# Three FFN norms with the reciprocal root applied where the gate and up products are read, and the opening's squares taken from token rows

## The chip, the core and the metric

One Trainium2 chip, of which the kernel uses one core. The metric is the device time of one execution in microseconds (us); less is better. TensorE (PE) does the matmuls and has a granted clock of either 1.2 or 2.4 GHz (0.50 or 1.00 in the profile). VectorE (DVE), ScalarE (ACT) and GpSimd (POOL) do elementwise work, SyncE (SP) issues DMA. Each engine runs its own queue in order, and engines wait for each other through semaphores.

## What is computed

A two-layer transformer over 512 latent tokens and 256 context tokens, width 1024, all in float32. Each layer is FFN, token mix, FFN, each with an RMS norm and adaLN modulation in front:

```python
def rms_norm(x, w):
    y = x * rsqrt(mean(x * x, axis=-1) + 1e-6) * w
def modulate(h, shift, scale):
    return h * (1.0 + scale) + shift
def swiglu(h, w_in, w_out):
    gate, up = split(h @ w_in, 2)
    return (silu(gate) * up) @ w_out          # inner width 2816
# per layer; mod = silu(c) @ w_ada + b_ada gives nine vectors of width 1024 each for latent and context
h = h + 0.5 * mod[2] * swiglu(modulate(rms_norm(h, w0), mod[0], mod[1]), ...)   # norm 3*layer
h = h +       mod[5] * token_mix(modulate(rms_norm(h, w1), mod[3], mod[4]))     # norm 3*layer + 1
h = h + 0.5 * mod[8] * swiglu(modulate(rms_norm(h, w2), mod[6], mod[7]), ...)   # norm 3*layer + 2
```

Context tokens have their own modulation vectors. The last FFN (norm 5) has latent tokens only. The result is a last RMS norm of the latent tokens.

## The kernel before

**Layout.** The residual h lies transposed in SBUF: 128 partitions, KD = 8 tiles of the width, TOK = 768 tokens (0 to 511 latent, 512 to 767 context). A norm's output is a pair xhi, xlo (float32r, high part and remainder) of the same shape; an activation is ahi, alo, a weight tile raw becomes whi, wlo. Each product is three passes, whi x xhi, whi x xlo, wlo x xhi, each as one matmul of 512 columns and one of 256 (part_ 0 and 1), into the two banks of a PSUM tensor pg[s]. A *unit* is one output tile of 128 columns; units alternate between slots s = 0 and 1, each with its own pg, raw, whi and wlo.

**Phases** (`phases`): for each FFN two halves of (in, out): 11 steps of one gate unit (slot 0) and one up unit (slot 1) with 8 k-steps each (`unit`, L709), then 8 output tiles of 11 k-steps. The mix is "win" (16 units), `mix`, and "wo" (8 units). In front of the matmuls of a unit TensorE waits for the slot's weights (s_w) and for its pg to have been read (s_free).

**A step of an in phase.** ScalarE (L1414) applies Silu to pg[0] into gate and then makes whi for both slots (split_hi, L1155). VectorE multiplies gate by pg[1] (L1901), copies ahi (L1904), subtracts alo (L1906), and makes wlo (split_lo, L1493), one of them ahead of these and one behind.

**AdaLN pieces.** The later modulation vectors are computed beside the FFNs (ADA_STEPS): 61 of the in steps of norms 0, 2 and 3 (and 3 out steps) carry a piece of w_ada. VectorE multiplies and adds its 16 tiles (sum_ada, L1574 and L1577), eight ahead of the first wlo and eight behind it, and TensorE folds the result over the partitions behind the step's second unit (ada_fold, L724), for which it waits until the last sum. SP loads the piece in four parts, each when its buffer has been summed, in one queue with the weight loads.

**Norms.** Squares are made by ScalarE (square, L1164, square_part, L1176), summed by VectorE into rstd (L1504, L1621) and over the partitions by TensorE against ones (square_sums, L770). ScalarE forms the reciprocal root by Ln and Exp (root, L1235 and L1237; a table load L1248 in front). Then for each k: VectorE tnorm = h * acol * rstd (norm_scaled, L1632), ScalarE xhi = tnorm + shift (L1244), VectorE xlo = tnorm + shift - xhi (L1640).

**Around a norm.** The last pair of units of the phase before is made part by part (last_pair): both slots' 512 latent tokens first, so that their squares can be taken during the 256 context tokens of both slots; add_part (L1612) adds them to h. Then first_pair makes the first two units of the new phase as the k arrive: latent tokens of slot 0 and 1, k = 0 to 3 each, then k = 4 to 7 in turns, then the context tokens slot by slot (part_product, L776).

**Opening** (opening_pair, norm 0). x is transposed on TensorE (L740) and copied to h by ScalarE and VectorE in turns; squares and sums of the 8 k follow. The first 16 tiles of w_ada arrive in four large loads (ada_first0 to 3): for each, first_modulation (L751), a copy to part_first (copy_first, L1202 or L1527), first_fold (L758), read_first into mod and acol. TensorE's queue alternates them with the k-steps of the first unit pair.

**257 columns.** The position DFT (L887) streams rows of dft_sb that are 257 columns long and lie one behind the other; the channel DFT (L853) streams 256 columns. Both are plain float32.

## Time and profile before

| | us |
|---|---|
| median of three runs | 2743.12 (2735.91 to 2744.52) |
| the profiled execution | 2739.12 |
| its span (first to last instruction) | 2737.2 |
| TensorE busy | 2664.7, 97% |
| VectorE busy | 1521.2, 56% |
| ScalarE busy | 692.3, 25% |
| mean granted TensorE clock | 0.992 |

The profile is of one execution. Its page gives busy times by engine; the other views used below are windows (busy time of each engine in a stretch, with the granted clock, the DMA engines' busy share and the GB/s moved), timelines (instructions of one engine in order), and groups of instructions by line, with shapes kept apart. "Idle before" in brackets says how long an engine stood still before an instruction and what released it. Matmul starts are measured, their ends are modelled and overlap; distances between starts are what counts.

### The profile page before, as it was taken

The page shows a single profiled execution, that of the slowest core. Times are in us where ns is not written, and L with a number is a line of the kernel's source. Part 1 is how long each engine was busy: PE and PEld are TensorE (multiplying, and loading weights), DVE is VectorE, ACT ScalarE, POOL GpSimd, SP SyncE. Part 2 cuts the span into 40 slices and gives each one's busy share as a digit, 9 for nine tenths or more (in the row PEclk, how much of TensorE's full clock was granted, in tenths as well). Part 3 has the DMA queues.
Part 4 walks back from the last instruction along what each step waited for, and adds up shares of the span by engine and source line. Part 5 has one row for each costly group of instructions (what it writes and reads, how often), then busy time and mean ns, then how long its engine had stood idle before and what let it go on. Part 6 is the DMA issues. An engine that isn't in the chain of part 4 may idle for free.

```text
span 2737.2 us, 42267 instructions
## 1 busy us (share of the span) xinstructions
PE 2664.7 (97%) x15515; PEld 2290.5 (84%) x15515; DVE 1521.2 (56%) x2621; ACT 692.3 (25%) x1075; POOL 93.7 (3%) x211
## 2 busy tenths in 40 slices
PE   7999999999999999999999999999999989999998
PEld 4888888888877888888888888888887877888886
DVE  5776477534376477626763677247536465543333
ACT  4111111122256221111111311111113345422222
POOL 0000000000034000000000000000000022000000
PEclk8999999999999999999999999999999999999999
DMA  7877477412200177536762577257422200233332
GB/s 228 198 184 185 113 184 184 125 50 79 54 17 2 54 165 185 146 86 159 184 161 58 123 184 175 71 140 184 126 70 84 69 26 17 81 96 100 91 110 81
DMA packets 485795, 316.98 MB, mean 116 GB/s; under 512 B 30588, under 2 KB 483664, under 8 KB 485712
## 3 DMA queue, kind: packets, MB, share of 16 engines
q1 hardware_dynamic: 485712, 315.88, 45.2%
q8 instruction: 51, 0.84, 0.1%
q14 instruction: 32, 0.26, 0.0%
HBM read 313.73 MB, written 2.10 MB: 115 GB/s over the span
## 4 chain that ended last, share of the span: by engine, by line
PE 91%; DVE 4%; ACT 2%; issue 1%; POOL 1%; DMA 0%; SPq 0%; DVEq 0%; ACTq 0%; POOLq 0%
PE pg L709 79%; PE pg L776 4%; PE p L1047 1%; PE pn L1030 1%; PE pg L986 1%; PE p L724 1%; DVE xlo L1640 1%; DVE tnorm L1632 1%; PE pg L867 1%; ACT whi L1155 0%; DVE wlo L1493 0%; PE pg L991 0%; DVE probT L1847 0%; DVE mx L1854 0%; ACT xhi L1244 0%
## 5 line engine op out<-in xcount | busy, mean ns | idle before, releaser
L709 PE MATMUL pg<-xhi,whi 128*128 128x512 f32 (+1 forms) x2856 | 794.5, 347 | 4.1 <-DVE wlo L1493 4.0
L709 PE MATMUL pg<-xhi,wlo 128*128 128x512 f32 (+1 forms) x2856 | 788.6, 344 | 0.0
L709 PE MATMUL pg<-xlo,whi 128*128 128x512 f32 (+1 forms) x2856 | 787.1, 344 | 0.0
L1155 ACT CAST whi<-raw 128x1024 fp32r<-128x1024 f32 (+1 forms) x288 | 321.8, 1118 | 1060.2 <-PE pg L709 1045.9
L1493 DVE TENSOR_TENSOR wlo<-raw,whi 128x1024 fp32r<-128x1024 f32 (+1 forms) x288 | 377.6, 1311 | 350.5 <-ACT whi L1155 347.8
L709 PEld LDWEIGHTS pg<-xhi,whi 128*128 128x128 f32 x2856 | 451.3, 188 | 72.6 <-DVE wlo L1493 5.9
L709 PEld LDWEIGHTS pg<-xlo,whi 128*128 128x128 f32 x2856 | 450.4, 188 | 69.3
L709 PEld LDWEIGHTS pg<-xhi,wlo 128*128 128x128 f32 x2856 | 450.4, 188 | 68.9
L1577 DVE SCALAR_TENSOR_TENSOR part<-ada,cond,part 128x256 f32<-128x256 f32 x960 | 465.3, 485 | 32.7
L1703 DVE SCALAR_TENSOR_TENSOR h<-pg,gcol,h 128x512 f32 (+1 forms) x118 | 71.4, 639 | 442.3 <-PE pg L709 437.5
L709 PE MATMUL pg<-ahi,whi 128*128 128x512 f32 x1100 | 306.1, 346 | 0.0
L709 PE MATMUL pg<-ahi,wlo 128*128 128x512 f32 x1100 | 305.4, 346 | 0.0
L709 PE MATMUL pg<-alo,whi 128*128 128x512 f32 x1100 | 304.4, 345 | 0.0
L1414 ACT ACTIVATE gate<-pg 128x768 f32<-128x768 f32 (+1 forms) x88 | 66.8, 759 | 574.4 <-PE pg L709 574.0
L709 PEld LDWEIGHTS pg<-alo,whi 128*128 128x128 f32 x1100 | 174.0, 188 | 27.7
L709 PEld LDWEIGHTS pg<-ahi,whi 128*128 128x128 f32 x1100 | 174.2, 188 | 27.0
L709 PEld LDWEIGHTS pg<-ahi,wlo 128*128 128x128 f32 x1100 | 173.6, 188 | 26.8
L1901 DVE TENSOR_TENSOR gate<-gate,pg 128x768 f32<-128x768 f32 (+1 forms) x88 | 78.1, 888 | 136.8 <-PE pg L709 136.8
L776 PE MATMUL pg<-xhi,whi 128*128 128x256 f32 (+1 forms) x240 | 85.2, 355 | 9.1 <-DVE xlo L1640 5.6
L1906 DVE TENSOR_TENSOR alo<-gate,ahi 128x768 f32 (+3 forms) x88 | 78.5, 892 | 9.7
L776 PE MATMUL pg<-xlo,whi 128*128 128x256 f32 (+1 forms) x240 | 81.0, 338 | 0.0
L776 PE MATMUL pg<-xhi,wlo 128*128 128x256 f32 (+1 forms) x240 | 80.6, 336 | 0.0
(212 smaller groups left out, 1983.4 us busy)
## 6 DMA issues: line engine op xcount, KB each, us to landing
ada<-in_w_ada SPq DMA_DIRECT2D x512, 256.0 KB, 4.2
raw<-in_ffn_w_in SPq DMA_DIRECT2D x176, 512.0 KB, 3.9
raw<-in_ffn_w_out SPq DMA_DIRECT2D x64, 704.0 KB, 4.5
raw<-in_w_in SPq DMA_DIRECT2D x24, 512.0 KB, 3.8
ada_first<-in_w_ada SPq DMA_DIRECT2D x8, 1024.0 KB, 11.9
raw<-in_w_in SPq DMA_DIRECT2D x16, 256.0 KB, 3.5
raw<-in_w_o SPq DMA_DIRECT2D x16, 256.0 KB, 2.8
raw<-in_w_o SPq DMA_DIRECT2D x32, 128.0 KB, 2.9
```

Source lines behind the costliest of these rows:

```text
L709: last = nc.tensor.matmul(pg[s][:, p0:p1], w[:, s, k], v[:, k, p0:p1], start=(k == 0 and n == 0), stop=(k == kt - 1 and n == 2))
L724: last = nc.tensor.matmul(pa[1][:, 2 * b:2 * b + 2], part[:, b * P:(b + 1) * P], halves, start=True, stop=True)
L776: last = nc.tensor.matmul(pg[s][:, c0:c0 + p1 - p0], w[:, s, k], v[:, k, p0:p1], start=(k == 0 and n == 0), stop=(k == kt - 1 and n == 2))
L867: last = nc.tensor.matmul(pg[0][:, p0:p1], w[:, 0, k], v[:, k, p0:p1], start=(k == 0 and n == 0), stop=(k == KD - 1 and n == 2))
L986: nc.tensor.matmul(pg[q % 2][:, c0:SEQ], w, k[s][:, lo * P:(lo + nk) * P], start=first_, stop=False, skip_group_check=True)
L1155: nc.scalar.copy(whi[:, s, 0:nk], raw[:, s, 0:nk]).then_inc(s_whi[s], 1)
L1414: nc.scalar.activation(gate[:, 0:t], pg[0][:, 0:t], ACT.Silu).then_inc(s_free[0], 1)
L1493: nc.vector.tensor_sub(wlo[:, s, 0:nk], raw[:, s, 0:nk], whi[:, s, 0:nk].bitcast(f32)).then_inc(s_w[s], 1)
L1577: ins = nc.vector.scalar_tensor_tensor(part[:, :], ada[q][:, a], cond2[:, n:n + 1], part[:, :], ALU.mult, ALU.add)
L1703: last = nc.vector.scalar_tensor_tensor(hv, pg[s][:, p0:p1], gcol[:, col, v:v + 1].rearrange("p o v -> p (o v)"), hv, ALU.mult, ALU.add)
L1901: nc.vector.tensor_tensor(gate[:, 0:t], gate[:, 0:t], pg[1][:, 0:t], ALU.mult).then_inc(s_free[1], 1)
L1906: nc.vector.tensor_sub(lo, gate[:, 0:t], hi.bitcast(f32)).then_inc(s_a[m, hf], 1)
```

## The change

For the norms in front of three FFNs (POST = norms 0, 2 and 3):

- xhi and xlo now hold h * acol, without the reciprocal root and the shift: ScalarE makes xhi from h (scaled_hi), VectorE xlo (scaled_low). tnorm and the wait for the root go.
- xhi and xlo get two more columns, 768 and 769 (XB = 770), that hold the shift vectors of latent and context tokens. Each second matmul of a product covers 258 columns, and the products of the shifts come out as pg columns 768 and 769. Rows of xhi and xlo lie 776 instead of 768 columns apart.
- In an in step VectorE multiplies pg[0] by rstd into gate, copies the two extra columns to gbias and releases pg[0]; ScalarE applies Silu with gbias as bias, in two parts. VectorE copies the extra columns of pg[1], multiplies pg[1] by rstd into up and forms gate = (up + bias) * gate in two parts. ScalarE makes slot 0's whi ahead of the Silu.
- Norm 3: the first six k of xhi and xlo are made during the last pair of the out phase (EARLY_K). Norm 2: xhi and xlo are still read by w_o's last pair, so they are made behind its latent part.
- In both, square_sums of the context tokens moves behind the latent products of first_pair, and the roots move behind all scaling.
- Opening: ScalarE squares the six token tiles of x (128 tokens x 1024) with accumulation into ssq; VectorE multiplies the identity by ssq into rstd in two instructions, which square_sums reads. VectorE copies five of six transposed tiles, ScalarE the last. square_sums comes ahead of first_modulation(0); the roots come in the second quarter, ahead of copy_first(2).

```diff
@@ -409,9 +418,28 @@
...
+        POST = (0, 2, 3)
+        EARLY_K = {3: KD - 2}
...
+        def product_columns(m, t):
+            return TOK + 2 if m in POST else t
@@ -699,7 +727,7 @@
...
-                parts = [(0, SEQ)] + ([(SEQ, TOK)] if t == TOK else [])
+                parts = [(0, SEQ)] + ([(SEQ, t)] if t > SEQ else [])
                 last = None
...
@@ -815,21 +844,21 @@
...
                             last.then_inc(s_unit[s], 1)
-                        if part_ == 0 and (s, k) == (0, 1):
+                        if part_ == 0 and (s, k) == (order[-1] if m in POST else (0, 1)):
                             square_sums(m, 1)
...
-                first_modulation(0)
                 square_sums(0, 0)
                 square_sums(0, 1)
+                first_modulation(0)
                 first_fold(0)
...
                 for k in range(KD - 2):
-                    for part_, (p0, p1) in enumerate(norm_parts(0)):
+                    for part_, (p0, p1) in enumerate([(0, SEQ), (SEQ, XB)]):
                         pe.wait_ge(s_xn, xn_count(0, part_, k))
@@ -1186,15 +1215,16 @@
...
+            for tt in range(TOK // P):
+                act.wait_ge(s_x[tt // 2], 32)
+                if tt >= 2:
+                    act.wait_ge(s_sq, tt - 1)
+                nc.scalar.activation(sqjunk[tt % 2][:, :], xtok[:, tt, :], ACT.Square, accum_out=ssq[:, tt:tt + 1]
+                                     ).then_inc(s_sq, 1 if tt < TOK // P - 1 else KD - TOK // P + 1)
+            act.wait_ge(s_xT, TOK // P)
+            nc.scalar.copy(h[:, :, TOK - P:TOK], pg[1][:, :].rearrange("p (k t) -> p k t", k=KD)).then_inc(s_free[1], 1)
             split_hi(0, 0, 0)
             split_hi(0, 1, 0)
-            act.wait_ge(s_free[1], 1)
-            for k in range(KD):
-                square(0, k, k % 2, 1)
@@ -1226,6 +1256,18 @@
...
+            def scaled_hi(m, part_, k):
+                p0, p1 = norm_parts(m)[part_]
+                v = 1 if p0 >= SEQ else 0
+                nc.scalar.activation(xhi[:, k, p0:p1], h[:, k, p0:p1], ACT.Identity, scale=acol[:, k, v:v + 1]
+                                     ).then_inc(s_xh, 1)
+            def shift_columns_hi(m, k0, k1):
+                shift = m // 3 * MT + m % 3 * 3 * KD
+                nc.scalar.copy(xhi[:, k0:k1, TOK:XB], mod[:, shift + k0:shift + k1, 0:2])
             def norm(i, m):
...
+                if m == 0:
+                    for q in range(KD // 2):
+                        if q == 2:
+                            copy_first(2)
+                        act.wait_ge(s_coef, coef_count(0, 2 * q))
+                        shift_columns_hi(0, 2 * q, 2 * q + 2)
+                        for k in (2 * q, 2 * q + 1):
+                            scaled_hi(0, 0, k)
+                            scaled_hi(0, 1, k)
+                        if q == 1:
+                            nc.scalar.preload_act_table_set("natural_log_exp_and_others")
+                            root(0)
+                            root(1)
+                    return
+                if m in POST:
+                    if phases[i][0] == "wo":
+                        act.wait_ge(s_coef, coef_count(m, 0))
+                        for k in range(4):
+                            scaled_hi(m, 0, k)
+                        split_hi(i + 1, 0, 0)
+                        square_part(i, 1, 0)
+                        for k in range(4, KD):
+                            scaled_hi(m, 0, k)
+                        split_hi(i + 1, 1, 0)
+                        square_part(i, 1, 1)
+                        shift_columns_hi(m, 0, KD)
+                        for k in range(KD):
+                            scaled_hi(m, 1, k)
+                    else:
+                        split_hi(i + 1, 0, 0)
+                        square_part(i, 1, 0)
+                        scaled_hi(m, 1, KD - 2)
+                        split_hi(i + 1, 1, 0)
+                        square_part(i, 1, 1)
+                        scaled_hi(m, 1, KD - 1)
+                    nc.scalar.preload_act_table_set("natural_log_exp_and_others")
+                    root(0)
+                    root(1)
+                    return
                 nc.scalar.preload_act_table_set("natural_log_exp_and_others")
                 root(0)
...
@@ -1405,6 +1478,14 @@
...
+                        if m in POST:
+                            split_hi(nxt, 0, jn)
+                            act.wait_ge(s_free[0], read_value(i, f))
+                            nc.scalar.activation(gate[:, 0:SEQ], gate[:, 0:SEQ], ACT.Silu, bias=gbias[:, 0:1])
+                            nc.scalar.activation(gate[:, SEQ:TOK], gate[:, SEQ:TOK], ACT.Silu, bias=gbias[:, 1:2]
+                                                 ).then_inc(s_gd, 1)
+                            split_hi(nxt, 1, jn)
+                            return
                         act.wait_ge(s_unit[0], f + (j0 + 1))
@@ -1438,8 +1519,19 @@
...
                     else:
-                        square_part(i, 0, 0)
-                        square_part(i, 0, 1)
+                        nn = next_norm(i)
+                        early = EARLY_K.get(nn, 0)
+                        if early:
+                            act.wait_ge(s_coef, coef_count(nn, 0))
+                            for part_ in range(2):
+                                if part_:
+                                    shift_columns_hi(nn, 0, KD)
+                                for k in range(early):
+                                    scaled_hi(nn, part_, k)
+                        for s in range(2):
+                            square_part(i, 0, s)
+                            if early:
+                                scaled_hi(nn, 0, early + s)
                 else:
@@ -1511,13 +1603,16 @@
...
             nc.vector.tensor_copy(window_r[:, :, :], window_sb[:, :].rearrange("p (a k) -> p a k", a=2))
...
+            for tt in range(TOK // P - 1):
                 dve.wait_ge(s_xT, tt + 1)
-                nc.vector.tensor_copy(h[:, :, tt * P:(tt + 1) * P], pg[1][:, :].rearrange("p (k t) -> p k t", k=KD)
-                                      ).then_inc(s_xTr[1] if tt < 4 else s_free[1], 1)
-            for k in range(KD):
-                sum_squares(0, k, k % 2)
+                nc.vector.tensor_copy(h[:, :, tt * P:(tt + 1) * P], pg[tt % 2][:, :].rearrange("p (k t) -> p k t", k=KD)
+                                      ).then_inc(s_xTr[tt % 2] if tt < 4 else s_free[0], 1)
+            for b, (t0_, t1_) in enumerate(((0, SEQ // P), (SEQ // P, TOK // P))):
+                dve.wait_ge(s_sq, (SEQ // P, KD)[b])
+                nc.vector.tensor_tensor(rstd[:, t0_ * P:t1_ * P].rearrange("p (a t) -> p a t", t=P),
+                                        ident.unsqueeze(1).broadcast_to([P, t1_ - t0_, P]),
+                                        ssq[:, t0_:t1_].unsqueeze(2).broadcast_to([P, t1_ - t0_, P]), ALU.mult
+                                        ).then_inc(s_acc, KD // 2 + 1)
             split_lo(0, 0, 0)
@@ -1641,6 +1736,21 @@
...
+            def scaled_low(m, part_, k):
+                p0, p1 = norm_parts(m)[part_]
+                v = 1 if p0 >= SEQ else 0
+                dve.wait_ge(s_xh, xn_count(m, part_, k))
+                nc.vector.scalar_tensor_tensor(xlo[:, k, p0:p1], h[:, k, p0:p1], acol[:, k, v:v + 1],
+                                               xhi[:, k, p0:p1].bitcast(f32), ALU.mult, ALU.subtract).then_inc(s_xn, 1)
...
             def norm_context(m, k0, k1):
@@ -1664,16 +1774,40 @@
...
                         read_first(q)
...
+                        scaled_low(0, 0, 2 * q)
+                        shift_columns_low(0, 2 * q, 2 * q + 2)
+                        scaled_low(0, 1, 2 * q)
+                        scaled_low(0, 0, 2 * q + 1)
                         if q == 0:
                             copy_first(1)
-                        low(0, 2 * q + 1)
-                        low(1, 2 * q + 1)
+                        scaled_low(0, 1, 2 * q + 1)
+                    return
+                if m in POST:
+                    if phases[i][0] == "wo":
+                        for k in range(3):
+                            scaled_low(m, 0, k)
+                        add_part(i, 1, 0)
+                        split_lo(i + 1, 0, 0)
+                        scaled_low(m, 0, 3)
+                        sum_part(m, 1, 0)
+                        for k in (4, 5):
+                            scaled_low(m, 0, k)
+                        add_part(i, 1, 1)
+                        split_lo(i + 1, 1, 0)
+                        for k in (6, 7):
+                            scaled_low(m, 0, k)
+                        sum_part(m, 1, 1)
+                        shift_columns_low(m, 0, KD)
+                        for k in range(KD):
+                            scaled_low(m, 1, k)
+                    else:
+                        split_lo(i + 1, 0, 0)
+                        sum_part(m, 1, 0)
+                        add_part(i, 1, 1)
+                        scaled_low(m, 1, KD - 2)
+                        split_lo(i + 1, 1, 0)
+                        sum_part(m, 1, 1)
+                        scaled_low(m, 1, KD - 1)
                     return
@@ -1884,23 +2018,48 @@
...
                 if kind == "in":
+                    if m in POST:
+                        dve.wait_ge(s_r, 2 * m + 2)
                     def step(f, nxt, jn, b):
...
                             sum_ada(b, f, 1)
+                        if m in POST:
+                            if not isinstance(f, int) or f:
+                                dve.wait_ge(s_a[m, hf], f)
+                            elif hf:
+                                dve.wait_ge(s_a[m, 0], HALF)
+                            dve.wait_ge(s_unit[0], f + (j0 + 1))
+                            nc.vector.tensor_tensor(gate[:, :], pg[0][:, 0:TOK], rstd[:, :], ALU.mult)
+                            nc.vector.tensor_copy(gbias[:, 0:2], pg[0][:, TOK:XB]).then_inc(s_free[0], 1)
                         split_lo(nxt, 0, jn)
...
                         dve.wait_ge(s_unit[1], f + (j0 + 1))
-                        dve.wait_ge(s_free[0], read_value(i, f))
+                        if m not in POST:
+                            dve.wait_ge(s_free[0], read_value(i, f))
                         col = slice(f, f + 1) if isinstance(f, int) else ds(f, 1)
...
                         lo = alo[:, col, 0:t].rearrange("p o t -> p (o t)")
-                        nc.vector.tensor_tensor(gate[:, 0:t], gate[:, 0:t], pg[1][:, 0:t], ALU.mult
-                                                ).then_inc(s_free[1], 1)
-                        dve.wait_ge(s_free[1], read_value(i, f))
+                        if m in POST:
+                            nc.vector.tensor_copy(gbias[:, 2:4], pg[1][:, TOK:XB])
+                            u = up[:, col, :].rearrange("p o t -> p (o t)")
+                            nc.vector.tensor_tensor(u, pg[1][:, 0:TOK], rstd[:, :], ALU.mult).then_inc(s_free[1], 1)
+                            dve.wait_ge(s_free[1], read_value(i, f))
+                            dve.wait_ge(s_gd, gate_count(m, hf, f))
+                            for v, (p0, p1) in enumerate(((0, SEQ), (SEQ, TOK))):
+                                last = nc.vector.scalar_tensor_tensor(gate[:, p0:p1], u[:, p0:p1],
+                                                                      gbias[:, 2 + v:3 + v], gate[:, p0:p1],
+                                                                      ALU.add, ALU.mult)
+                            last.then_inc(s_gm, 1)
+                            dve.wait_ge(s_gm, gate_count(m, hf, f))
+                        else:
+                            nc.vector.tensor_tensor(gate[:, 0:t], gate[:, 0:t], pg[1][:, 0:t], ALU.mult
+                                                    ).then_inc(s_free[1], 1)
+                            dve.wait_ge(s_free[1], read_value(i, f))
                         nc.vector.tensor_copy(hi, gate[:, 0:t]).then_inc(s_ahi[m, hf], 1)
@@ -1942,10 +2101,19 @@
...
                         coefficients(nn)
+                        early = EARLY_K.get(nn, 0)
+                        for part_ in range(2):
+                            if early and part_:
+                                shift_columns_low(nn, 0, KD)
+                            for k in range(early):
+                                scaled_low(nn, part_, k)
                         for s in range(2):
...
                             sum_part(nn, 0, s)
-                        add_part(i, 1, 0)
+                            if early:
+                                scaled_low(nn, 0, early + s)
+                        if early or nn not in POST:
+                            add_part(i, 1, 0)
                 else:
```

## Rows read from the trace of the kernel before

**Rows 1.** The page, busy time of each engine (share of the span) and instructions

```profile
PE 2664.7 (97%) x15515; PEld 2290.5 (84%) x15515; DVE 1521.2 (56%) x2621; ACT 692.3 (25%) x1075; POOL 93.7 (3%) x211
```

**Rows 2.** Windows: stretch, its us, busy us of each engine, clock, DMA share, GB/s

```profile
134.16:151.25 17.09, 17.09 (x101) 15.00 (x102) 12.36 (x23) 2.79 (x4) 0.00 (x0) 1.00 0.75 184
```

**Rows 3.** The chain that ended last: start us, us, what (the two DFTs)

```profile
684.09 1.73 PE p L853 x8
...
2203.43 3.47 PE pn L887 x16
```

**Rows 4.** Timeline of VectorE in one adaLN step

```profile
144.40 1.23 DVE L1493 TENSOR_TENSOR wlo<-raw,whi 128x1024 fp32r<-128x1024 f32 x1 [2.69 <-ACT whi L1155]
145.54 4.13 DVE L1577 SCALAR_TENSOR_TENSOR part<-ada,cond,part 128x256 f32<-128x256 f32 x8
150.95 0.95 DVE L1901 TENSOR_TENSOR gate<-gate,pg 128x768 f32<-128x768 f32 x1 [1.27 <-PE pg L709]
```

**Rows 5.** VectorE groups by line and shape: count, busy us, mean ns, idle before

```profile
L1584 DVE TENSOR_TENSOR mod<-p,bias 128x4 f32 x59 | 9.2, 155 | 0.0
...
L1612 DVE SCALAR_TENSOR_TENSOR h<-pg,gcol,h 128x512 f32<-128x512 f32 x8 | 6.0, 751 | 31.6 <-PE pg L776 31.6
L1612 DVE SCALAR_TENSOR_TENSOR h<-pg,gcol,h 128x256 f32<-128x256 f32 x12 | 5.8, 481 | 11.6 <-PE pg L776 11.6
```

**Rows 6.** Timeline of ScalarE in the same adaLN step

```profile
142.62 0.81 ACT L1414 ACTIVATE gate<-pg 128x768 f32<-128x768 f32 x1 [7.67 <-PE pg L709]
143.33 1.04 ACT L1155 CAST whi<-raw 128x1024 fp32r<-128x1024 f32 x1
```

**Rows 7.** Timeline of TensorE in the opening

```profile
24.85 3.64 PE L751 MATMUL p<-ada_first,cond 128*32 128x512 f32 x16 [5.90 <-DMA ada_first<-in_w_ada]
29.97 2.93 PE L770 MATMUL pn<-rstd,ones 128*128 128x512 f32 x4 [1.48 <-DVE rstd L1504]
32.69 1.71 PE L758 MATMUL p<-consts,part_first 128*128 128x2 f32 x8
...
37.89 0.80 PE L776 MATMUL pg<-xhi,whi 128*128 128x512 f32 x1
...
59.02 0.50 PE L776 MATMUL pg<-xhi,whi 128*128 128x512 f32 x1 [0.70 <-DVE xlo L1640]
...
65.63 0.61 PE L709 MATMUL pg<-xhi,whi 128*128 128x512 f32 x2 [1.01 <-DVE wlo L1493]
```

**Rows 8.** Timeline of ScalarE in the opening

```profile
28.64 0.57 ACT L1202 COPY part_first<-p 128x512 f32<-128x512 f32 x1
29.22 1.28 ACT L1248 ACT_TABLE_LOAD   x1
...
33.83 0.42 ACT L1237 ACTIVATE rstd<-rstd 128x256 f32<-128x256 f32 x1
```

**Rows 9.** Windows, opening and start of m=2; the clock follows the POOL column

```profile
25.00:30.00 5.00, 3.52 (x17) 0.53 (x13) 4.58 (x6) 4.33 (x6) 0.00 (x0) 0.50 1.10 349
956.00:958.00 2.00, 1.45 (x4) 0.72 (x3) 2.00 (x3) 1.03 (x2) 0.00 (x0) 0.50 0.56 168
```

**Rows 10.** ScalarE groups by line and shape

```profile
L1244 ACT ACTIVATE xhi<-tnorm,mod 128x512 fp32r<-128x512 f32 x40 | 28.7, 718 | 27.8 <-DVE tnorm L1632 27.8
L1244 ACT ACTIVATE xhi<-tnorm,mod 128x256 fp32r<-128x256 f32 x52 | 25.7, 506 | 16.4 <-DVE tnorm L1632 16.1
```

**Rows 11.** Timeline of TensorE from w_o to the second FFN (m=2)

```profile
951.63 0.28 PE L776 MATMUL pg<-xhi,wlo 128*128 128x256 f32 x1
953.97 0.51 PE L776 MATMUL pg<-xhi,whi 128*128 128x512 f32 x1 [2.06 <-DVE wlo L1493]
...
975.70 0.62 PE L709 MATMUL pg<-xhi,whi 128*128 128x512 f32 x2 [0.22 <-DVE wlo L1493]
```

**Rows 12.** Timeline of TensorE from layer 0 to layer 1 (m=3)

```profile
1520.95 0.28 PE L776 MATMUL pg<-ahi,wlo 128*128 128x256 f32 x1
...
1542.89 0.62 PE L709 MATMUL pg<-xhi,whi 128*128 128x512 f32 x2 [0.31 <-DVE wlo L1493]
```

70 lines of the change are left out of this document (36 added, 34 removed).

## Prediction

> **What bounds the kernel now.** I read the page's busy shares first: TensorE is busy for 97% of the span [rows 1], so the time is TensorE's work plus the few places where it stands still or runs at half clock. An edit pays only there. The next view is one step of the gate/up loop with an adaLN piece in it (windows): 17.09 us, TensorE busy for all of it, VectorE for 12.36 [rows 2]. Last come the timelines around the three places where a norm precedes an FFN: the opening (m=0), the step from w_o to the second FFN (m=2) and from layer 0 to layer 1 (m=3). There TensorE waits, and twice it runs at 1.2 instead of 2.4 GHz. The change touches exactly three kinds of place: these norms, the opening's squares, and the 66 gate/up steps behind the norms (3 norms, 2 halves, 11 column tiles).
>
> **Two extra columns (a loss).** Each second matmul of an xhi or xlo product has 258 columns instead of 256. There are 66 steps x 2 units x 8 k x 3 = 3168 of them. The price per column: 16 passes of 257 columns take 3.47 us, 216.9 ns each, where 8 passes of 256 take 1.73 us, 216.3 ns each [rows 3]; those are passes at two cycles a column, and L887 streams rows of dft_sb that lie 257 columns apart, so neither the uneven width nor an odd row start shows a step. Two columns at 2.4 GHz are 0.83 ns, and I take 3168 x 0.83 ns = **2.6 us**. Below that I see no reason; upwards the two rows leave 1 ns or so per matmul, 2 to 4 us in all.
>
> **VectorE in the 66 steps (covered).** Per step it gains a multiply of the gate by the root (a second L1901, 0.95 us [rows 4]), two copies of two columns and two scalar_tensor_tensor (512 and 256 tokens); the multiply by the up half takes the place of the old one. The copies are nearest to a read of 4 columns out of PSUM, 0.155 us each. The two others are nearest to L1612, 0.75 and 0.48 us, which reads PSUM; they could be a tenth less, or pay the handoff (0.15 us) once more [rows 5]. Sum: 0.95 + 2 x 0.155 + 0.75 + 0.48 = 2.5 us (bounds 2.3 and 3.0), and 0.3 for two more waits on its own results. 61 of the 66 steps also have an adaLN piece, the fullest case: 12.36 + 2.5 = 14.9 of 17.1 us.
>
> Order matters more than the sum, because VectorE's queue is in order and TensorE's fold of the piece waits for the last of its sums. Now: the first unit ends at about 142.5, wlo runs at 144.40 behind ScalarE's Silu and whi, the last eight sums at 145.54 to 149.67, and it then waits 1.27 us for the second unit [rows 4, 6]. After: the new instructions sit behind the second unit and push ahi, alo, wlo and the first eight sums by 1.4 us, so that these end at about 143.1 instead of 141.7; the gate multiply follows until 144.0. ScalarE now does whi before the Silu, ready at 143.7, so wlo starts at 144.1, no later than before. The last sums end at about 149.4 and the fold (at 150.75) is not late. What is queued behind the new wait on the Silu (gate_done): ahi, alo, the second wlo, due only 8.4 us after the unit's end. SP's queue: the second weight load and two of the four adaLN loads go out 1.4 us later and are used a step later; DMA engines are 75% busy [rows 2]. The cover is 1.4 us at the fold and 1.8 us over the whole step; past it TensorE waits in 61 steps.
>
> The Trainium skill speaks against this part: "VectorE: DVE Perf Modes", section "The TRN2 errata", charges each instruction a fixed cost (58 cycles from SBUF, 120 from PSUM, besides one per element), so five more instructions per step should weigh by their number. By its figures, called an estimate, the same five make (888 + 122 + 122 + 570 + 314)/0.96 GHz = 2.1 us. The trace's small PSUM read is dearer than its 0.127 us, and the sum goes by the rows; by either the cover holds.
>
> **The opening (gain 4.2 us).** Before, ScalarE and VectorE take 8.4 us in turns over eight squares and sums; the ones product starts at 29.97, the first fold at 32.69, the first modulation behind it lasts 3.64 us as the one at 24.85 does, and the first product starts at 37.89 [rows 7]. Afterwards the squares are six ScalarE instructions during the transposes, and two short VectorE ones; the ones product should end by 22, before anything else needs TensorE. Late next is the DMA: the first modulation waits for ada_first at 24.85 as now and ends at 28.5. ScalarE copies it (0.57 us, at 28.64 now too [rows 8]), the fold starts at 29.3 instead of 32.7, and all behind it moves by **3.4 us**. The second piece of ada_first must have landed by 31.0: 2.1 MB more at the 349 GB/s of that stretch make 24.85 + 6.0 = 30.9 [rows 9], just in time. xhi and xlo no longer wait for the root.
>
> Then come eight k-steps at TensorE's own pace, with one new delay: in the second quarter ScalarE runs a table load (1.28) and four root instructions (about 2.2) [rows 8] before copy_first(2), for which the fold on TensorE waits. Counted from the fold before: coefficients at +1.4, four scaled_hi until +3.8 (0.72 and 0.51, overlapping [rows 10]), roots until +7.5, copy until +8.1, against a fold due at +7.1: **1.0 us lost** (bounds 0 and 1.5). In the last quarter a k needs ScalarE and VectorE once each, not VectorE twice: so of the 0.70 us wait at 59.02 and the like ones behind it [rows 7] I keep 0.6. In front of 65.63 TensorE has waited 1.01 us for wlo, because ScalarE did the Silu and its table load first; with whi first I keep 0.75. From the last fold's k=5 (ends at about 58.2) to 65.63 are 7.5 us, after it 5.6: **1.9 gained**. Together 3.4 + 1.9 - 1.0 = 4.3, rounded down to 4.2.
>
> **m=2 (gain 5.7 us).** The last product of w_o is issued at 951.63, ends its columns at 951.75, and the second unit pair starts at 975.70: 23.95 us [rows 11]. The work in it is that of a step: 17.09, less its fold of 0.35 and plus the ones product of 0.43, say 17.2. So 6.7 us are lost: 2.06 idle at 953.97, small waits, and half clock (granted 0.50 at 956 to 958 [rows 9]). After: no root ahead of xhi. ScalarE can scale from 946.8, when slot 1's early part is added and squared; four scaled_hi at 0.63 apart, then whi of slot 0 until 950.4, wlo until 951.6: slot 0 starts without a wait. Slot 1 is behind four more scaled_hi: whi 953.3 to 954.3, wlo until 955.5, due at 954.6. I keep 1.0 us of idle time and expect the clock to stay up, since half of today's idle time is left; the next rows of xhi and xlo are out before they are needed. 23.95 - 18.2 = **5.7**; if the clock falls all the same, 3.
>
> **m=3 (gain 4.4 us).** The same stretch is 1521.07 to 1542.89, 21.8 us [rows 12]. Six of eight k are now made during the last pair of the out phase, when VectorE and ScalarE idle (xhi and xlo aren't read there): 6 x (0.67 + 0.43) = 6.6 us on each, beginning at 1501.6, done at 1508.7, before slot 1's part at 1512.5. Left is slot 1's split behind the last product, some 0.5 + 1.05 + 1.2 us against four k of slot 0, 2.7 us: 0.2 kept. 21.8 - 17.4 = **4.4**. In both pairs the last part is slot by slot, so the next unit's split (0.5 + 1.05, VectorE's multiply beside it, 1.15) fits the 2.9 us of slot 1.
>
> **Sum.** 4.2 + 5.7 + 4.4 - 2.6 = 11.7 us. The profiled execution took 2739.1 (span 2737.2), so 2727.4; it lies 4 us under the median of the three runs, 2743.1 (2735.9 to 2744.5), from which it would be 2731.4. I predict **2730**.
>
> **The rivals.** (a) TensorE stays at full clock in the opening, as the ones product moves into its idle time from 19 to 24.9. The modulation would take 1.9 instead of 3.64 us, but the second piece still lands at 30.9; the product starts at 32.8, and k=0 runs at 2.4 GHz: 2 to 3 us more, 2727. Against: with the transposes until 19 the clock is at half from 25 to 30 [rows 9], and the ones product fills only 1.5 us of the time between. Chance 0.13. "TensorE: Matmul & The Clock Gate", section "Why this matters for your kernels" of the Trainium skill, asks for no long idle gaps; how it decides between (a) and the forecast no row here shows.
> (b) The boundaries keep more than I say: clock down at m=2 (2.7 us), the fold at +7.1 and m=3's slot 1 each a little later, 4 to 7 us in all: 2734 to 2737. For it: half clock after only 2.06 us of idle time. Chance 0.17.
> (c) Slower: VectorE becomes the bound of the 61 adaLN steps. It decides from 4.7 us of added work and waits per step (17.09 - 12.36, against my 2.8, less 0.2 of waits that exist): each 0.1 us past that costs 6.1 us, and 0.2 us past it undoes the gain. With 0.35 past it, 61 x 0.35 = 21 us: 2752. For it: DMA fills 75% of the step and the new instructions are the longest kind. Against: 1.8 us of cover. Chance 0.08.
> (d) The columns cost more, as by an unaligned row of 3104 bytes: past 4.5 ns per matmul the gain is gone; at 8 ns 25 us, 2753. Rows 3 speak against it. Chance 0.03.
> (e) The change doesn't do what it says, say a split that stays behind a wait as before: no difference, 2741. Chance 0.04.
>
> **How the numbers follow.** The forecast (2725 to 2734) has 0.55. Its lower end and (a) reach 2722, (b) ends at 2738; I close the range at 2722 to 2739, which leaves out (c), (d), (e) and tails, under 0.2. A measurement of this kernel can tell 0.3%, 8.2 us, from no change: faster means under 2734.9. That is the forecast, (a) and a little of (b), 0.70; same 0.19; slower 0.11.
>
> **What would show it.** Right: adaLN steps of 17.1 to 17.2 us with VectorE at 14.7 to 15; first fold at about 29.3 and first product at 34.5; the unit behind the opening at 61.4; 18.2 and 17.4 us at m=2 and m=3. Wrong: steps over 17.2, a fold that waits for L1577's line, granted clock 0.5 behind m=2, or 258-column matmuls over 1 ns longer.

## The result

The changed kernel is not faster. Its median is 2743.4 us (2740.8 to 2749.1, 20 runs), that of the kernel before beside it 2740.5 us (2735.7 to 2747.0, 20 runs); the ratio is 1.0013 with a 95% interval of 1.0007 to 1.0019. Forecast were 2730 us (2722 to 2739), a gain of 0.4%. The profiled execution took 2740.8 us with a span of 2739.1, where that of before took 2739.1 us with a span of 2737.2: the spans differ by 1.9 us.

The page of the changed kernel, busy time of each engine, answers to [rows 1]:

```profile
PE 2674.8 (98%) x15515; PEld 2296.1 (84%) x15515; DVE 1633.3 (60%) x2904; ACT 714.3 (26%) x1149; POOL 93.4 (3%) x211
```

TensorE issues as many matmuls as before (15515) and is busy 10 us longer: it stands still less, and its matmuls take longer. The two halves of the story can be seen apart. First the gains, in the timeline of TensorE in the opening after the change [rows 7]:

```profile
25.56 3.27 PE L779 MATMUL p<-ada_first,cond 128*32 128x512 f32 x16 [3.64 <-DMA ada_first<-in_w_ada]
29.55 1.05 PE L786 MATMUL p<-consts,part_first 128*128 128x2 f32 x8 [0.71 <-ACT part_first L1232]
31.57 3.52 PE L779 MATMUL p<-ada_first,cond 128*32 128x512 f32 x16 [0.96 <-DMA ada_first<-in_w_ada]
35.02 0.56 PE L804 MATMUL pg<-xhi,whi 128*128 128x512 f32 x1
...
44.97 1.05 PE L786 MATMUL p<-consts,part_first 128*128 128x2 f32 x8 [0.37 <-ACT part_first L1232]
...
60.27 0.61 PE L737 MATMUL pg<-xhi,whi 128*128 128x512 f32 x2 [0.34 <-DVE wlo L1585]
```

The waits for VectorE in front of single k (0.70 us at 59.02 before) are gone, and the wait for wlo in front of the unit behind the opening has fallen from 1.01 to 0.34 us. What is late now is the DMA of ada_first, twice (3.64 and 0.96 us). The unit behind the opening starts at 60.27 instead of 65.63: 5.4 us.

The chain of the changed kernel from w_o into the second FFN, and from layer 0 to layer 1 (start us, us, what):

```profile
934.31 11.17 PE pg L804 x48
...
955.48 8.64 PE pg L804 x36
...
970.32 16.87 PE pg L737 x96
...
1493.94 17.86 PE pg L804 x90
...
1529.28 5.77 PE pg L804 x48
1535.05 10.08 PE pg L737 x57
```

In the chain of before the same two stretches begin at

```profile
934.41 13.78 PE pg L776 x72
...
1497.47 17.87 PE pg L776 x90
```

and end at 975.70 and 1542.89 [rows 11, 12]. So m=2 took 41.3 us and takes 36.0, 5.3 less; m=3 took 45.4 and takes 41.1, 4.3 less. The clock at m=2 stays up; the window that had 0.50 [rows 9] now reads

```profile
956.00:958.00 2.00, 2.00 (x10) 1.59 (x10) 2.00 (x7) 2.00 (x6) 0.00 (x0) 1.00 0.64 183
```

The gains make 5.4 + 5.3 + 4.3 = 15.0 us, against 14.3 forecast. Yet the changed kernel enters w_o's last pair only 0.1 us ahead (934.31 against 934.41), though it left the opening 5.4 ahead. Between the places where it gains, it loses. Two looped steps of the gate/up phase in the chain of the changed kernel:

```profile
130.20 16.96 PE pg L737 x96
147.17 0.34 PE p L752 x4
147.51 16.96 PE pg L737 x96
```

and one of the kernel before:

```profile
1061.61 16.75 PE pg L709 x96
1078.37 0.34 PE p L724 x4
```

The same 96 matmuls and the same fold of 0.34 us, but 16.96 instead of 16.75 us. The view of windows over that step, with each engine's busy time, answers to [rows 2]:

```profile
147.51:164.82 17.31, 17.31 (x102) 15.25 (x102) 14.56 (x28) 3.23 (x5) 0.00 (x0) 1.00 0.75 181
```

TensorE is busy for all 17.31 us at full clock. It waits for nobody; its matmuls are slower. The last FFN (m=5) shows it most plainly, since no norm, no root and no extra column was changed there. Its stretch in the chain, before and then after:

```profile
2373.13 348.47 PE pg L709 x1536
```

```profile
2369.53 354.40 PE pg L737 x1536
```

5.9 us more for 1536 equal matmuls. The view of windows for TensorE counts the matmuls at work in a stretch; in 20 us of a gate/up half the kernel before has 90, the changed one 88:

```profile
2400.00:2420.00 20.00, 20.00 (x90) 1.00 0.36 103
```

```profile
2400.00:2420.00 20.00, 20.00 (x88) 1.00 0.31 89
```

From one start to the next, averaged over the records of this stretch, a 512-column matmul on xhi or xlo takes 226.7 ns before and 232.5 after; on ahi or alo, which the change leaves alone, 226.7 and 226.8. That points at the one thing which xhi and xlo have got everywhere: rows of 776 in place of 768 columns, 3104 bytes instead of 3072.

The ledger, from the first matmul of each phase in the two traces: gains 15.0; lost in the six gate/up halves with a changed norm 12.2 (2.7, 2.3, 1.6, 2.0, 1.6, 2.1); lost in the last FFN 5.9; in the token mix of layer 1 ahead of it 1.0; regained in m=1 1.1, in the out halves 0.8 and behind the last FFN 0.4. 12.2 + 5.9 + 1.0 - 15.0 - 1.1 - 0.8 - 0.4 = 1.8, where the spans differ by 1.9. The out halves, which the change doesn't touch, are a sum of both signs: two of them lost 1.3 us each, two gained 1.7 and 1.8.

### The profile page after: what moved, and what is told of

It is laid out like the page before. It is cut to its first block, busy times and chain, and to the rows that moved or that the text cites. A ratio compares the mean times of both kernels' runs of the same rounds, so it can differ in the third digit from the quotient of the medians.

```text
span 2739.1 us, 42548 instructions
## 1 busy us (share of the span) xinstructions
PE 2674.8 (98%) x15515; PEld 2296.1 (84%) x15515; DVE 1633.3 (60%) x2904; ACT 714.3 (26%) x1149; POOL 93.4 (3%) x211
## 4 chain that ended last, share of the span: by engine, by line
PE 92%; DVE 3%; ACT 2%; issue 1%; DMA 1%; SPq 1%; POOL 1%; ACTq 0%; DVEq 0%; POOLq 0%
PE pg L737 80%; PE pg L804 5%; PE p L1076 1%; PE pn L1059 1%; PE pg L1015 1%; PE p L752 1%; PE pg L896 1%; DMA ada_first<-in_w_ada 0%; PE pg L1020 0%; DVE wlo L1585 0%; DVE probT L1981 0%; DVE xlo L1735 0%; ACT whi L1184 0%; PE p L882 0%; DVE tnorm L1727 0%
## 5 line engine op out<-in xcount | busy, mean ns | idle before, releaser
L737 PE MATMUL pg<-xhi,whi 128*128 128x512 f32 (+2 forms) x2856 | 799.7, 348 | 2.3 <-DVE wlo L1585 2.0
L737 PE MATMUL pg<-xhi,wlo 128*128 128x512 f32 (+2 forms) x2856 | 794.6, 347 | 0.0
L737 PE MATMUL pg<-xlo,whi 128*128 128x512 f32 (+2 forms) x2856 | 793.9, 346 | 0.0
L1585 DVE TENSOR_TENSOR wlo<-raw,whi 128x1024 fp32r<-128x1024 f32 (+1 forms) x288 | 377.4, 1311 | 166.1 <-ACT whi L1184 162.5
L2048 DVE COPY gbias<-pg 128x2 f32<-128x2 f32 x66 | 10.5, 160 | 131.8 <-PE pg L737 130.7
L804 PE MATMUL pg<-xhi,whi 128*128 128x512 f32 (+2 forms) x240 | 83.7, 349 | 4.4 <-DVE xlo L1735 2.4
L2035 DVE TENSOR_TENSOR gate<-pg,rstd 128x768 f32<-128x768 f32 x66 | 62.8, 952 | 33.7 <-PE pg L804 19.6
L804 PE MATMUL pg<-xlo,whi 128*128 128x512 f32 (+2 forms) x240 | 80.0, 333 | 0.0
L804 PE MATMUL pg<-xhi,wlo 128*128 128x512 f32 (+2 forms) x240 | 79.7, 332 | 0.0
```

What stands on the lines that cost most here:

```text
L737: last = nc.tensor.matmul(pg[s][:, p0:p1], w[:, s, k], v[:, k, p0:p1], start=(k == 0 and n == 0), stop=(k == kt - 1 and n == 2))
L804: last = nc.tensor.matmul(pg[s][:, c0:c0 + p1 - p0], w[:, s, k], v[:, k, p0:p1], start=(k == 0 and n == 0), stop=(k == kt - 1 and n == 2))
L1585: nc.vector.tensor_sub(wlo[:, s, 0:nk], raw[:, s, 0:nk], whi[:, s, 0:nk].bitcast(f32)).then_inc(s_w[s], 1)
L2035: nc.vector.tensor_tensor(gate[:, :], pg[0][:, 0:TOK], rstd[:, :], ALU.mult)
```

## The experiments

Steps are compared by the chain's entry "x96" for the 96 matmuls between two folds at m=2. "A pair" is a 512-column matmul and the narrower one behind it, start to start, as a mean over the gate/up halves of m=0, 2 and 3. Where a run's name says 3328 or 3104, that is the row pitch of xhi and xlo in bytes. There is one trace for each kernel. The runs of the fold matmul on the kernel before, the run of widths and the last run of the fold are single executions. Of an edit that has several places the main one is shown, with "..." for the rest.

**The pitch alone, in the kernel before.** All that lies in the rows of xhi and xlo moves with them.

```diff
+        XW = TOK + 8
...
-        xhi = place("xhi", [P, KD, TOK], f32r, start["xhi"])
-        xlo = place("xlo", [P, KD, TOK], f32r, start["xlo"])
+        xhi = place("xhi", [P, KD, XW], f32r, start["xhi"])
+        xlo = place("xlo", [P, KD, XW], f32r, start["xlo"])
...
```

> The kernel before with one thing changed: rows of xhi and xlo lie 776 instead of 768 columns apart (3104 instead of 3072 bytes), 8 unused columns behind each row. In the changed kernel the 1056 matmuls of 512 columns that read xhi or xlo in the last FFN start 232.5 ns apart, in the kernel before 226.7, though the change does nothing to them. Theory (row pitch): the pitch alone does this. Then this kernel shows 232 to 233 ns there, about 350 ns instead of 346.6 for a pair (512 and 256 columns) in the FFN in phases, and is 12 to 20 us slower than the kernel before. Rival (the two extra columns and what they bring): the pitch costs nothing, and the time is that of before within 3 us.

2759.1 us, ratio 1.0074 (1.0057 to 1.0091). Its step and its last FFN in the chain:

```profile
1065.36 16.90 PE pg L711 x96
...
2386.84 354.38 PE pg L711 x1536
```

The last FFN has 232.5 ns, exactly that of the changed kernel. Nothing but the pitch and the addresses behind the two buffers is changed here, and the next run shows that the addresses cost nothing. The run is about 20 us longer: 2.5 ns a pair x 3168 = 8, the last FFN 6, out halves that were slower in this run 3 (351.6 against 349.2 ns a pair), and some 3 that I can't assign. The first two, 14 us, are the pitch's by these means; the out halves don't read xhi or xlo, and in the next run they were as slow (351.4) at the old pitch.

**The addresses behind them, without the pitch.** xhi and xlo keep 3072 bytes per row; everything placed behind each moves by 256 bytes.

```diff
-        sizes = dict(h=KD * TOK * 4, xhi=KD * TOK * 4, xlo=KD * TOK * 4, ahi=HALF * TOK * 4,
+        sizes = dict(h=KD * TOK * 4, xhi=KD * TOK * 4 + 256, xlo=KD * TOK * 4 + 256, ahi=HALF * TOK * 4,
```

> The kernel before with the tensors behind xhi moved up as the change moves them (xlo and ahi's neighbours by 256 and 512 bytes), row pitch unchanged at 3072 bytes. If the start addresses and not the pitch slow the matmuls, it shows the 232.5 ns of the last FFN and 12 to 20 us more; by the pitch theory it keeps 226.7 ns and the time of before within 3 us.

2739.7 us, ratio 1.0000 (0.9989 to 1.0011), 226.7 ns in the last FFN, 16.75 us in the step. A shift of the buffers by 256 bytes doesn't matter.

**No extra columns, in the changed kernel.** The shift is then missing in the result.

```diff
-            return TOK + 2 if m in POST else t
+            return t
...
```

> The changed kernel with products of 256 instead of 258 columns: the shift is left out of the result (the two PSUM columns are read unwritten). Theory (row pitch): the pitch stays, so it stays slow; only 2 columns x 3168 matmuls x 0.417 ns = 2.6 us are saved (2 to 5 us). Rival (extra columns): pairs return to 346.6 ns, the in step to 17.1 us, and it is 14 us or more faster than the changed kernel.

2743.3 us, ratio 1.0021 (1.0011 to 1.0031). The step falls from 16.96 to 16.88 us and a pair from 351.1 to 349.3 ns, the last FFN stays at 232.5, and out halves that ran slower (352.4 against 348.5 ns a pair, some 5 us) hide even that: the 2 to 5 us expected from the missing columns didn't show in the time. The columns explain 1.8 of the 4.1 ns that a pair has lost; the pitch the rest.

**Another pitch, 3136 bytes.**

```diff
-        XB, XW = TOK + 2, TOK + 8
+        XB, XW = TOK + 2, TOK + 16
```

> The changed kernel with row pitch 784 columns = 3136 bytes, a multiple of 64, where 3104 is one of 32 only. If the start of a row within 64 bytes is what costs, odd rows are whole again: in step 17.13 us, last FFN 226.7 ns, time 2727 to 2731. If what costs is the row's place against a larger unit (the pitch 3072 is a multiple of 512 and so is that of the weights), it stays between: 2735 to 2745.

2755.4 us, ratio 1.0068 (1.0052 to 1.0085):

```profile
1044.91 17.06 PE pg L737 x96
```

The time is above both of the expected ranges. A multiple of 64 bytes doesn't help: the last FFN has 231.7 ns. Phase here is the place of a row's start within a larger unit of bytes. In the last FFN the distances of the starts form a fixed pattern, which at 3136 bytes repeats after 4 k, 4 x 64 = 256 bytes of phase, and at 3104 only with the unit's 8 k, 8 x 32 = 256. That gave the next pitch to try.

**3328 bytes, 13 x 256.** To make room, the decay table and the condition's columns moved into unused parts of the weight buffers, and two instructions on the table are done in halves. The edit of the changed kernel; the kernel before gets the same pitch:

```diff
-        XB, XW = TOK + 2, TOK + 8
+        XB, XW = TOK + 2, TOK + 64
...
```

> The changed kernel with the rows of xhi and xlo 3328 bytes apart (13 x 256) in place of 3104; the two extra columns stay. To make room, the decay table and the condition's columns lie in unused parts of the weight buffers, and Exp and the identity's addition work on the table in two halves. Pitch as a multiple of 256 bytes (row phase): the 512-column matmuls on xhi and xlo in the last FFN go back from 232.5 to 226.7 ns, an adaLN step from 17.31 to about 17.15 us, and the gains of opening, m=2 and m=3 stay: 2722 to 2731 us, faster than before by 0.3 to 0.6%. Any pitch other than 3072 costs: 2743 or more, as the changed kernel or the pitch of 3136 (2755).

> The kernel before with the rows of xhi and xlo 3328 bytes apart, and the decay table and the condition's columns moved as in the changed kernel of that pitch. Pitch as a multiple of 256 bytes: 226.7 ns in the last FFN and the time of before, 2738 to 2741 us. Any pitch other than 3072 costs: 2750 to 2760 us. If the moved tables or the halved instructions cost something of their own, it shows here, with the matmuls at 226.7 ns and the time over 2742 us.

The kernel before at 3328 takes 2738.3 us, ratio 0.9992 (0.9983 to 1.0001), with 226.7 ns in the last FFN: this pitch is free, and so is the move. The changed kernel at 3328 takes 2747.8, ratio 1.0022 (1.0013 to 1.0031). Its last FFN is cured (348.51 us in the chain, 226.7 ns), but its steps got worse. The chain of each, the kernel before first:

```profile
1060.53 16.75 PE pg L711 x96
```

```profile
1060.52 17.07 PE pg L737 x96
```

353.5 against 346.9 ns a pair. My expectation of 2722 to 2731 failed: something beyond the pitch costs up to 6.6 ns a pair. The pitch of 3136 bytes had steps of nearly this length too (17.06), so those needn't be the price of the pitch alone.

**The weights' rows.** If the phase of a moving row against its weight row counted, weight rows of 544 bytes (512 + 32) beside moving rows of 3104 would cure the pitch.

```diff
+        WP = 136
+        whx = [place(f"whx{s}", [P, KD, WP], f32r, start["whi"] + s * HALF * P * 4) for s in range(2)]
...
```

> The changed kernel, xhi and xlo at 3104 bytes as it has them, but the weight tiles of the phases over eight k written at a row pitch of 544 bytes (512 + 32), so that a moving row and its weight row shift together by 32 bytes per k. If what matters is the phase of a moving row against its weight row, the 512-column matmuls go back to 226.7 ns and the time to about 2727 us. If the moving rows' own addresses matter, they stay at 232.5 ns and the time at 2743 us, or it is longer by what the weight rows' new pitch costs.

> The kernel before, xhi and xlo at 3072 bytes, with the same weight rows at a pitch of 544 bytes. By the relative phase its 512-column matmuls on xhi and xlo go from 226.7 to about 232 ns and the time to about 2755 to 2759 us, as with its rows of 3104 bytes. By the moving rows' own addresses nothing changes: 2738 us, or the weight rows show a cost of their own.

In the changed kernel 2745.5 us (ratio 1.0018, 1.0009 to 1.0027), 230.3 ns in the last FFN: not cured. In the kernel before 2751.9 us (1.0034, 1.0021 to 1.0047), 231.4 ns and

```profile
1066.44 16.89 PE pg L716 x96
```

with its moving rows still 3072 bytes apart. So the relative phase is refuted (by the first of the two: the second alone, at 231.4 ns, would fit it), and the rows of either operand can slow the stream by themselves.

**Is it the columns' width?** The changed kernel at 3328 without the extra columns, the shift again missing in the result:

> The changed kernel at the pitch of 3328 bytes with the two extra columns left out of every product (256 columns in the second matmul of a pair in place of 258; the shift is missing in the result). Theory now: the extra columns cost a whole step of the matmul's time, 353.5 against 346.9 ns per pair, 6.6 ns x 3168 = 21 us of the 2747.8 of the run with them: without them pairs of about 347 ns in the FFNs and a time of 2725 to 2730 us. Rival: the pairs of 353.5 ns are a state into which this kernel falls whatever its columns, as the out halves do in places: pairs stay at 353 and the time at 2745 or more.

2749.7 us, ratio 1.0037 (1.0024 to 1.0051), and

```profile
1061.31 17.07 PE pg L737 x96
```

The theory that the extra columns cost these 6.6 ns fell: with 256 columns a pair takes 353.1 ns here, and 346.9 in the kernel before with the same pitch. The stream falls into one of two rhythms, called cadences below. It can be seen in the kernel before too: its out half of m=2 from 1160 to 1240 us holds 455 matmuls and that of the changed kernel 463, windows of TensorE, before and after:

```profile
1160.00:1240.00 80.00, 80.00 (x455) 1.00 0.32 82
```

```profile
1160.00:1240.00 80.00, 80.00 (x463) 1.00 0.34 84
```

353.3 against 346.7 ns a pair, for a whole half, at full clock and with no wait. At the pitches of 3072 and 3328 bytes nearly every step on 256 columns has one of two lengths, 16.75 or 17.07 us.

**Widths.** A first try ran without its second matmuls (2556.3 us) and says nothing of widths; the second, in which the result means nothing:

> The kernel before at the pitch of 3328 bytes with other widths in the looped pairs: the second matmul of a pair has 250 and 258 columns (the two in-halves of m=0), 260 and 272 (m=2), 264 and 280 (m=3), read from column 448 on, and the last FFN's matmuls 500 and 496 in place of 512 in its two in-halves. The result means nothing. If a matmul's time is linear at 0.42 ns a column, pairs beside 346.7 ns for 256: 250 344.2, 258 347.5, 260 348.3, 264 350.0, 272 353.3, 280 356.7; alone 500 221.7 and 496 220.0 ns. If it goes in steps of 16 columns: 258, 260, 264 and 272 all 353.3, 280 360.0, 250 346.7; alone 500 226.7, 496 220.0. If a state locks whatever the columns: values of either level without order by width.

Means per pair, with the second matmul at: 250 columns 350.9 ns, 258 353.2 (behind its first step), 260 353.2, 264 350.1, 272 about 358, 280 359.9. Alone: 500 columns 226.7, 496 220.0 ns. The single matmuls go in a step (500 costs as much as 512, 496 a step of 6.7 ns less), the pairs follow neither the line nor the steps: 250 columns cost more than 264. With 258 columns only the first step of the half went at 346.7 ns a pair, and all steps behind it had 17.07 us, but the run without extra columns has that length too. Each width has one half in one execution, so this run doesn't part the price of a width from the cadence.

**The restart's phase.** At each fold TensorE's stream stops and starts anew. One of the fold's two small matmuls is issued twice or three times; the result is the same, and neither VectorE nor ScalarE is touched.

```diff
-                for b in range(2):
+                for b in (0, 0, 1):
                     last = nc.tensor.matmul(pa[1][:, 2 * b:2 * b + 2], part[:, b * P:(b + 1) * P], halves,
```

> The kernel before at the pitch of 3328 bytes (2738.3 us, pairs of 346.9 ns) with the same fold matmul issued twice. Phase: the cadence may change to 353.3 ns in all adaLN steps (2765 to 2775 us) or stay (2745 to 2752 us); which of the two can't be said beforehand. VectorE's work: it stays at 346.9 ns for certain.

> The kernel before at the pitch of 3328 bytes with one fold matmul issued three times (twice gave a step's 96 matmuls of 17.06 us in place of 16.75). If the restart's phase sets the cadence, the 96 matmuls take 16.75 or 17.06 us in a whole half, and either can come; 16.75 in the adaLN steps would show that the cost of the run with two is no effect of more matmuls: 2738 + 61 x 0.45 = 2765 us at 16.75, 2782 at 17.06. If each repeated matmul delays the stream behind it, the 96 take 17.06 or more.

The kernel before at 3328, chains at m=2: the fold with its matmul once, twice, three times. One more costs 0.22 us in front of the restart:

```profile
1077.27 0.34 PE p L726 x4
```

```profile
1083.68 0.56 PE p L726 x6
```

```profile
1071.40 0.79 PE p L726 x8
```

The steps with the matmul twice, at m=0 and m=2, and then three times, at m=2:

```profile
132.62 16.75 PE pg L711 x96
...
1066.61 17.06 PE pg L711 x96
```

```profile
1072.19 16.75 PE pg L711 x96
```

Once: 16.75 us in 55 of the 58 looped steps that the chain shows whole; the other three are the first behind each norm. Twice: 16.75 at m=0 and 17.06 in the steps of m=2 and m=3, 2765.6 us. Three times: 16.75 in all but the same three, and 2764.6 us in spite of 61 x 0.22 = 14 us more in folds than with twice. So 0.22 us more in front of the restart can change the length of all steps behind, and as much again changes it back; at m=0 the first 0.22 us changed nothing. Both are single executions, but the ten executions with the matmul once reach 2744.0 us at most, and 14 us of folds on top of that make 2758, not 2765.6.

> The run without extra columns at the pitch of 3328 bytes (2749.7 us, pairs of 353.5 ns), with one of the fold's two small matmuls issued twice, so that PE's stream restarts some 112 ns later in each adaLN step: 61 x 0.22 = 14 us at most more work if the repeated one costs twice its 112 ns. If the phase of the restart sets the cadence, pairs go to 346.9 ns in all or most of the adaLN steps and 21 us come back, less the added matmuls: 2736 to 2743 us. If the extra VectorE work sets it, pairs stay at 353 and the time rises to 2757 to 2764.

> The changed kernel without extra columns at the pitch of 3328 bytes, with one fold matmul issued three times (once: 17.07 us for a step's 96 matmuls; twice: 17.06 in m=2, though not in all halves). Phase: 16.75 us in at least one half, and up to 20 us off what the added matmuls cost, 2750 + 27 = 2777 us: 2757 to 2777. If VectorE's added work sets the slow cadence, 17.06 in every half.

The changed kernel without columns at 3328, matmul twice:

```profile
130.90 16.75 PE pg L737 x96
...
1058.29 17.06 PE pg L737 x96
```

Its m=0, which had 17.07 or more in every step with the matmul once, now has 16.75 in all but its first; m=2 and m=3 stay at 17.06. The median is 2750.7 us, ratio 1.0053 (1.0030 to 1.0075), between the two expectations. Of the 13.6 us that the repeated matmuls add, all but 1.1 came back in the traced execution, 5.3 of it to be read off in the gate/up halves (351.4 instead of 353.1 ns a pair) and 3 in the out halves, where I had hoped for 21. The five executions don't agree, however: three took 2749.3 to 2750.7 us and two 2761.1. With all of the 13.6 us and nothing back it would be 2763.3, so it may be that the same kernel has its fast steps in one execution and not in the next; no trace was taken of a long one. Three times: 2776.0 us, 17.07 in nearly all steps (16.75 in three), no half at 16.75: that is what was expected if VectorE's added work sets the length, and not if the phase alone does. Two other runs speak against VectorE's work: it is in the m=0 that has 16.75, and it is not in the kernel before that has 17.06. So it is neither enough for the slow length nor needed. Without influence it isn't shown to be: single steps of 16.75 in the changed kernel fall back at the next fold, and those of before don't.

**Breaking the cadence.** In the looped steps the extra columns are in the product whi x xhi alone, so that one pair in three has 258 columns. The shift is then taken at the precision of the high parts.

```diff
-                        for p0, p1 in parts:
+                        for p0, p1 in [(0, SEQ)] + ([(SEQ, min(t, TOK) if n else t)] if t > SEQ else []):
...
```

> The changed kernel at the pitch of 3328 bytes with the two extra columns in one of the three products of a k alone, whi x xhi, in the looped steps (the shift is then taken at the products' single precision part). By the step of 6.6 ns for a pair with 258 columns: one pair in three has it, 7 us in place of 21, and the time is 2747.8 - 14 = 2733 us, faster than before by 0.2 to 0.3%. If any pair of 258 columns throws its neighbours too, all stay at 353 and the time at 2745 or more.

> The changed kernel at its own pitch of 3104 bytes, with the extra columns in the product whi x xhi alone. By the pitch: the last FFN stays at 232.5 ns and the pairs at about 350 ns, so 2743.4 less at most the columns' 1.8 ns x 2112 = 4 us: 2739 to 2743 us, no faster than before. If breaking the cadence were what made the same edit 20 us faster at 3328 bytes, it is below 2735 here too.

At 3328 it is 2727.9 us (2726.1 to 2729.2), ratio **0.9956** (0.9943 to 0.9970), the fastest of all:

```profile
1037.75 16.79 PE pg L736 x96
...
1054.87 16.86 PE pg L736 x96
```

It is 5 us under what was expected, and hardly for the reason expected: that was a price of 6.6 ns for every pair with 258 columns, and the run without them had no faster pairs. Its looped steps alternate between these two lengths in every half and never get to 17.07; the last FFN takes 348.49 us. Against the run with all columns at 3328 a step gains 0.25 us, 16 us over 66 steps, and the out halves 3.3 ns x 1374 pairs, 4.5 us; measured are 19.9. At 3104 the same edit gives 2746.3 us, ratio 1.0022 (1.0013 to 1.0032), a step of 16.92 and 232.5 ns in the last FFN. That is above the 2739 to 2743 expected: its out halves, which the edit doesn't touch, had 353.0 ns a pair where the changed kernel's have 348.6, some 6 us. Of what was tried only both together pay: a pitch that is free, and a pattern of widths that didn't settle in the slow cadence.

## Why the prediction was wrong

**The step that failed** is the first term, "Two extra columns (a loss)". It charged 0.83 ns for each of 3168 matmuls, 2.6 us. Measured in those six halves are 12.2 us, 3.9 ns a pair, and 5.9 + 1.0 us more behind them, in matmuls that the term didn't count at all. By the runs at 3104 bytes 1.8 ns of a pair are the columns' and 2.4 the pitch's. Two mistakes lie in it. It asked what two more columns cost and not what a longer row costs: the pitch belongs to the buffer, and every reader of xhi and xlo pays, the untouched last FFN included. And its witness was unfit: the 257-column passes of [rows 3] run at two cycles a column, 216.9 ns for half the columns of a 226.7 ns matmul. A stream at half rate may hide a row whose start costs a few ns; that is my reading, and no run here tests it.

**Rival (d)** named the right mechanism, "an unaligned row of 3104 bytes", and its threshold of 4.5 ns was close: at 3.9 ns in the loops and 5.8 ns in the last FFN the gain is gone. I gave it 0.03, on the strength of [rows 3] alone. Its result of 2753 was for 8 ns.

**The opening** (4.2 us) gained 5.4, more than forecast although its first part gained less. The first fold was forecast for 29.3 and came at 29.55, the first product for 34.5 and came at 35.02, since ada_first's second piece landed at 31.5 and not at 30.9. The delay by the roots that I put at 1.0 us shows as a wait of 0.37 at 44.97; with it the unit started at 60.27, not 61.4. In the last quarter no wait for scaling is left, where 0.6 us were kept. The clock was at full between the two modulations but at half under the second (3.52 us), so rival (a) did not come about.

**m=2** (5.7) gained 5.3, and from the last product of w_o to the second unit pair it takes 18.5 us for the 18.2 forecast: 0.70 us of idle time in place of the 1.0 kept, with the clock at 1.00 as expected, and the eight k at the slower rate of the new rows. **m=3** (4.4) gained 4.3. Rival (b) did not come about either.

**VectorE in the steps** was costed at 14.9 us and has 14.56. The order held as well. VectorE of the changed kernel in one step, its last sums and the next wait:

```profile
157.04 0.15 DVE L2036 COPY gbias<-pg 128x2 f32<-128x2 f32 x1
157.22 1.22 DVE L1585 TENSOR_TENSOR wlo<-raw,whi 128x1024 fp32r<-128x1024 f32 x1
158.36 4.12 DVE L1672 SCALAR_TENSOR_TENSOR part<-ada,cond,part 128x256 f32<-128x256 f32 x8
164.51 0.16 DVE L2048 COPY gbias<-pg 128x2 f32<-128x2 f32 x1 [2.03 <-PE pg L737]
```

The sums end at 162.5, the fold comes at 164.48, so 2.0 us of cover are left, and rival (c) did not come about. The small copies took 0.15 and 0.16 us, as taken from the 0.155 of [rows 5]. By the fixed cost in the Trainium skill's "VectorE: DVE Perf Modes", section "The TRN2 errata", they would take an estimated 0.127 us; the trace decides, and by either the cover held.

**What would show it** did its work: "steps over 17.2" (17.31) and "258-column matmuls over 1 ns longer" (1.8) were two of the marks named as wrong, and the first is in the first windows that one opens.

The last level, why a step on these buffers falls into 16.75 or 17.07 us, is shown only so far: 0.22 us of matmul in front of the restart can change it. What in the chip has the two cadences, why a row of 3104 bytes costs time at all, and what pushes the changed kernel's steps back to the slow cadence, stays open. So it also stays open how much of the changed kernel's own 16.96, at a pitch where neither length appears, is pitch and how much would be cadence; without its columns the two kernels there differ by 0.02 us (16.88 and 16.90).

## What to carry to other kernels

When a bound TensorE stream reads a buffer, the pitch of its rows is part of the matmul's price: keep it at a value that was measured to be free (here 3072 or 3328 bytes for the moving rows, 512 for the weights'), and pad up to the next such value (128 bytes of phase weren't tried) rather than to the smallest that fits. Before costing an edit that lengthens a row, list all who read the buffer, and take the price from matmuls of the same rate. After a change to a saturated stream, compare the same count of matmuls far away from the edit first: one row of the chain (x1536, 348.47 against 354.40) finds what no wait shows. And before an edit is judged by a few us, look at the cadence of the stretches that it doesn't touch: the out halves alone moved these kernels by up to 6 us.

## What was not expected of the hardware

- A row pitch of 3104 or 3136 bytes slows a 512-column matmul from 226.7 to 232.5 or 231.7 ns, at full granted clock, without a wait, in a pattern that repeats with 256 bytes of phase; a pitch of 544 in place of 512 bytes for the weights does so too (231.4). 3072 and 3328 are free. 128 bytes of phase weren't tried.
- The Trainium skill's "TensorE: Matmul & The Clock Gate", section "Back-to-back issue gap", gives N/2.4 + 2.5 ns for a matmul of N columns by itself, 215.8 for 512 (an estimate by its formula), and about 131 ns for one of 512 in a stream with weight loads; neither has a term for the rows. The traces here differ from both: 226.7 ns for 512 columns of float32r with a weight load each, as much for 500, and 220.0 for 496.
- 512 and 256 columns in turn have two cadences, 353.3 and 346.7 ns a pair, and mostly keep one for whole halves (455 or 463 matmuls in 80 us). 0.22 us in front of a restart can change it for the steps behind, in this kernel some 13 us; no view of waits shows it.
